# Banded attention's queries as block products, and a block's last modulation sums moved into a feed-forward

## The reference, cut to what matters

```
cond = silu(c)
for i in range(2):
    mod = cond @ w_ada[i] + b_ada[i]                       # 6 x 1024 values
    sh1, sc1, gt1, sh2, sc2, gt2 = split(mod, 6)
    h = rmsnorm(x, g_mix[i]) * (1 + sc1) + sh1
    y = mla(h, ...) if i == 0 else swa(h, ...)
    x = x + gt1 * y
    h = rmsnorm(x, g_mlp[i]) * (1 + sc2) + sh2
    x = x + gt2 * (square(relu(h @ w_ff1[i])) @ w_ff2[i])

def swa(h, w_qkv, b_qkv, sinks, w_o, b_o):
    qkv = h @ w_qkv + b_qkv      # 1024 query columns, 256 of keys, 256 of values
    ...                          # scores in a band of 128 tokens, ALiBi bias, sinks, softmax, values
    return o @ w_o + b_o
```

## Time and profile before

| | |
|---|---|
| three runs, us | 3033.01, 3033.98, 3034.07 |
| span of the profiled execution, us | 3027.7 |
| TensorE busy | 2908.8 us, 96% |
| VectorE busy | 1656.7 us, 55% |
| ScalarE busy | 722.1 us, 24% |
| GpSimd busy | 71.7 us, 2% |
| mean granted TensorE clock | 0.991 of 2.4 GHz |
| transfers | 451.73 MB, mean 149 GB/s |

### The profile page before, as it was taken

How to read it: one execution, slowest core, us unless ns; L and a number is a source line. 1 busy time by engine, 2 the same in 40 slices (tenths; PEclk the granted TensorE clock), 3 DMA queues, 4 the chain that set the end, 5 groups by cost and what they waited for, 6 DMA issues and landing times.

```text
span 3027.7 us, 36246 instructions
## 1 busy us (share of the span) xinstructions
PE 2908.8 (96%) x14418; PEld 2184.0 (72%) x14418; DVE 1656.7 (55%) x2729; ACT 722.1 (24%) x1393; POOL 71.7 (2%) x136
## 2 busy tenths in 40 slices
PE   7999999999899999989999999999999998999998
PEld 5988888788557888844444434478888846888887
DVE  4777887365666677621111157464555467655545
ACT  4444444220672001111011022420000116200001
POOL 0000000000000111000000001000000020000000
PEclk9999999999999999999999999999999999999999
DMA  5100111021103555379999967012222270122221
GB/s 236 70 36 35 65 41 56 35 91 56 67 12 104 211 184 219 118 326 421 422 422 422 422 265 319 28 56 84 84 84 84 112 279 29 56 84 93 101 85 56
DMA packets 71751, 451.73 MB, mean 149 GB/s; under 512 B 8032, under 2 KB 10224, under 8 KB 24112
## 3 DMA queue, kind: packets, MB, share of 16 engines
q1 hardware_dynamic: 53840, 374.17, 30.9%
q0 software_dynamic: 17040, 73.18, 6.7%
q10 hardware_dynamic: 720, 2.29, 0.2%
HBM read 445.41 MB, written 2.10 MB: 148 GB/s over the span
## 4 chain that ended last, share of the span: by engine, by line
PE 85%; DVE 8%; DVEq 2%; DMA 2%; ACT 2%; issue 1%; ACTq 0%; SPq 0%
PE PS L253 78%; PE PS L1671 1%; PE PS L1556 1%; PE PS L1654 1%; DVE arena L1621 1%; DVE stat L1680 1%; DVEq L1124 1%; DMA hT<-stream 1%; PE PS L2451 1%; DMA ring<-stream 1%; DMA arena<-x 1%; PE PS L2431 1%; ACT arena L1574 0%; DVE arena L1120 0%; DVE PS L2782 0%
## 5 line engine op out<-in xcount | busy, mean ns | idle before, releaser
L253 PE MATMUL PS<-arena 128*128 128x256 f32 (+3 forms) x4960 | 982.6, 388 | 17.0 <-DVE arena L1162 8.5
L253 PEld LDWEIGHTS PS<-arena 128*128 128x128 f32 (+1 forms) x4960 | 742.8, 183 | 232.4 <-issue 146.9
L253 PE MATMUL PS<-arena,ring 128*128 128x256 f32 (+1 forms) x1992 | 466.9, 390 | 0.0
L253 PEld LDWEIGHTS PS<-arena,ring 128*128 128x128 f32 x1992 | 377.8, 190 | 73.8 <-issue 25.5
L253 PE MATMUL PS<-hT,ring 128*128 128x256 f32 (+1 forms) x1504 | 400.6, 421 | 7.2 <-ACT hT L420 6.2
L253 PEld LDWEIGHTS PS<-hT,ring 128*128 128x128 f32 x1504 | 284.4, 190 | 110.5 <-issue 77.9
L253 PE MATMUL PS<-xT,arena 128*128 128x256 f32 x1056 | 232.4, 379 | 0.0
L253 PEld LDWEIGHTS PS<-xT,arena 128*128 128x128 f32 x1056 | 200.5, 190 | 31.5 <-issue 4.8
L2203 DVE TENSOR_TENSOR arena<-arena,PS 128x512 f32<-128x512 f32 x16 | 11.0, 687 | 370.1 <-PE PS L253 370.1
L253 PE MATMUL PS<-hT,arena 128*128 128x256 f32 (+1 forms) x864 | 195.1, 442 | 0.8 <-DMA hT<-stream 0.8
L597 DVE CUSTOM_DVE_ANT_0 arena<-arena,PS 128x1024 f32<-128x1024 f32 x128 | 152.1, 1217 | 43.0 <-DMA arena<-adat 41.2
(11 more groups left out here) (312 smaller groups left out, 3018.3 us busy)
## 6 DMA issues: line engine op xcount, KB each, us to landing
ring<-stream SPq DMA_DIRECT2D x217, 1024.0 KB, 7.1
arena<-stream SPq DMA_DIRECT2D x98, 1024.0 KB, 18.3
arena<-adat POOLq DMA_DIRECT2D x88, 512.0 KB, 4.9
hT<-stream SPq DMA_DIRECT2D x32, 1024.0 KB, 18.7
arena<-adat POOLq DMA_DIRECT2D x20, 1024.0 KB, 10.8
arena<-stream SPq DMA_DIRECT2D x8, 512.0 KB, 4.4
arena<-x ACTq DMA_DIRECT2D x4, 512.0 KB, 15.3
xT<-stream SPq DMA_DIRECT2D x2, 1024.0 KB, 20.9
```

The source lines that it names most:

```text
L253: ins = nc.tensor.matmul(out_, lhsT, rhs, start=start, stop=stop_, **kw)
```

## The change

Two things are changed.

The projection of banded attention does its keys and values first, as plain products (two key tiles, two of values), and then the queries as two quads (numbers N_SQ and N_SQ + 1, with the activations' differences T_s). ScalarE writes one corner of each with its bias, VectorE the other three (`query_ends`). The stream's units are put in that order. The bias table of attention (16 small instructions) moves from the start of `swa_qkv_dve` to behind the middle sums of the second query quad.

Stage 3 of the modulation rows moves into the end of layer 0's feed-forward: VectorE does 9, 10, 9 and 4 steps in its quads 12, 13, 14 and 15, between the next quad's weight sums and the accumulation. The four buffers move to the place of the first weight's activation differences, which are done with by then, and GpSimd issues the first tile when twelve quads are done, all 32 ahead of the two constant loads. The condition row is no longer made a second time: ScalarE copies stage 2's row out of PSUM into SBUF (`cond_act`, in latent attention's projection), and stages 2 and 3 read that.

Beside that, the three attentions share one set of eight semaphores, with counts that go on from one to the next.

```diff
-           [24064 + 2048 * i for i in range(4)], [23040 + 1024 * i for i in range(4)])
-MOD_DIAG = (27648, 5120, 22016, 21504)
+           [24064 + 2048 * i for i in range(4)], [20480 + 1024 * i for i in range(4)])
+MOD_DIAG = (27648, 5120, 22016)
...
+        cond = pt[:, :, :].rearrange("p a b -> p (a b)")
+        def cond_act(act):
+            act.wait_ge(m_sum, 3)
+            act.wait_ge(x_ok, 2)
+            nc.scalar.activation(cond, PS[:, MOD_BANK[2]:MOD_BANK[2] + 2, :].rearrange("p a b -> p (a b)"), ACT.Copy)\
+                .then_inc(m_sum, 1)
         def mod_steps(v, st, i0, n):
-            if i0 == 0:
-                v.wait_ge(m_sum, st + 1)
+            if i0 == 0 and st < 3:
+                v.wait_ge(m_sum, st + 1 + st // 2)
...
-                row = PS[:, MOD_BANK[st]:MOD_BANK[st] + 2, :].rearrange("p a b -> p (a b)")
+                row = cond if st >= 2 else PS[:, MOD_BANK[st]:MOD_BANK[st] + 2, :].rearrange("p a b -> p (a b)")
...
             small_squares(act, 5, ckv, KVT)
+            cond_act(act)
             take(2)
...
+        N_LATE, LATE_STEPS = 12, (9, 10, 9, 4)
...
                 if n + 1 < QF:
                     weight_sums(v, q + 1, u + 2)
-                elif L == 0:
-                    mod_diag(v, 3)
+                if L == 0 and n >= N_LATE:
+                    i = n - N_LATE
+                    mod_steps(v, 3, sum(LATE_STEPS[:i]), LATE_STEPS[i])
                 v.drain()
...
         def swa_qkv_pe(pe):
-            pe.wait_ge(n_r, NR[8] + 2)
-            mod_sum(pe, 3)
-            for j in range(12):
-                g, su = G_SQKV + j, U_SQKV + 2 * min(j // 4, 2)
-                if j < 10:
-                    gemm(pe, g, g, su, 0, ((j % 4) * P,), hT, ready=NM[8] if j == 0 else None)
+            for j in range(4):
+                g = G_SQKV + j
+                if j < 2:
+                    gemm(pe, g, g, U_SQKV, 0, (j * P,), hT, ready=NM[8] if j == 0 else None)
                 else:
-                    t0 = (j - 10) * 2 * P
-                    gemm_tok(pe, g, g, su, hT, (t0, t0 + P), 256, 256)
-                if j in (3, 7, 11):
-                    pend[0] += 2
+                    t0 = (j - 2) * 2 * P
+                    gemm_tok(pe, g, g, U_SQKV, hT, (t0, t0 + P), 256, 256)
+            pend[0] += 2
+            pe.wait_ge(evac_done, G_SQKV + 4)
+            for n in (N_SQ, N_SQ + 1):
+                for i in range(1, 8):
+                    part_pe(pe, n, i)
+                quad_done(n)
             flush(pe)
...
+        def query_ends(v, n):
+            j = 4 * (n - N_SQ)
+            u0, u1 = part_u(n, 0), part_u(n, 1)
+            def biased(j0, cols, src):
+                for t in range(2):
+                    ins = nc.vector.scalar_tensor_tensor(qn[:, j0 + t, cols], u1[:, t, :],
+                                                         V[:, V_BQKV + j0 + t:V_BQKV + j0 + t + 1], src[:, t, :],
+                                                         ALU.add, ALU.add)
+                return ins
+            v.drain()
+            biased(j + 2, slice(HN, T), u0)
+            v.wait_ge(p_p, 7 * n + 6)
+            biased(j, slice(HN, T), part_bank(1)).then_inc(p_d, 1)
+            v.wait_ge(p_p, 7 * n + 7)
+            biased(j + 2, slice(0, HN), part_bank(2)).then_inc(p_d, 1)
         def swa_qkv_dve(v):
-            for n in range(16):
-                nc.vector.tensor_scalar(BT[:, n // 4, n % 4, :], C[:, C_DIST:C_DIST + 2 * P],
-                                        C[:, C_SLOPE + n:C_SLOPE + n + 1], None, ALU.mult)
-            mod_steps(v, 3, 0, 32)
+            v.wait_ge(n_mod, NM[8] + KT)
+            block_sums(v, hT, T_s)
+            sums_dve(v, N_SQ)
             mod_end(v, 3, ((6, 80, V_GMLP + 8),))
...
+            for n in (N_SQ, N_SQ + 1):
+                last_sum_dve(v, n)
+                mid_dve(v, n, 0)
+                mid_dve(v, n, 1)
+                if n == N_SQ:
+                    sums_dve(v, n + 1)
+                else:
+                    for i in range(16):
+                        nc.vector.tensor_scalar(BT[:, i // 4, i % 4, :], C[:, C_DIST:C_DIST + 2 * P],
+                                                C[:, C_SLOPE + i:C_SLOPE + i + 1], None, ALU.mult)
+                query_ends(v, n)
             v.drain().then_inc(v_ok, 1)
...
-            pool.wait_ge(q_p, 7 * 14)
-            tiles(96, 100)
+            pool.wait_ge(q_p, 7 * 12)
+            tiles(96, 128)
             pool.wait_ge(x_ok, 4)
             pool.dma_start(bvs, bv).then_inc(in_pool, 16)
             pool.dma_start(snk[:, 0, :], sinks).then_inc(in_pool, 16)
-            tiles(100, 128)
```

More of the change, by code:

```diff
@@ L56 @@
 N_MWO = N_OUT + 2
-N_SWO = N_MWO + 2
+N_SQ = N_MWO + 2
+N_SWO = N_SQ + 2
 V_SLOT = 6
@@ L682, in quad_out @@
             j = 4 * (n % 2)
-            return gt[:, j:j + 2, :], gt[:, j + 2:j + 4, :]
+            tiles = gt if n < N_SQ else qn
+            return tiles[:, j:j + 2, :], tiles[:, j + 2:j + 4, :]
         def quad_moving(n):
@@ L1516, in build, with attention @@
         MAX, NEGMAX, SUM, RECIP, SINK = range(5)
-        def attention(name, n, nh, score, chunk, dest, groups, value, outs, exp_io, norm_io, maximum, scale,
+        a_s, a_m, a_e, a_n, a_t, a_c, a_v, a_o = (sem(f"att_{x}") for x in
+            ("s", "m", "e", "n", "t", "c", "v", "o"))
+        def attention(u0, i0, o0, n, nh, score, chunk, dest, groups, value, outs, exp_io, norm_io, maximum, scale,
                       sink=False, beside=None):
-            a_s, a_m, a_e, a_n, a_t, a_c, a_v, a_o = (sem(f"{name}_{x}") for x in
-                ("s", "m", "e", "n", "t", "c", "v", "o"))
             col = lambda what, u: stat[:, what, u % 2, 0:nh]
@@ L1680, in gqa_maximum @@
             return nc.vector.tensor_reduce(neg, S[:, :, 0:HK], AX.XY, ALU.max, negate=True)
-        gqa_pe, gqa_act, gqa_dve, gqa_out, gqa_scores = attention(
-            "gqa", 64, 1, gqa_score, gqa_chunk, gqa_dest, [list(range(4 * i, 4 * i + 4)) for i in range(16)],
+        gqa_pe, gqa_act, gqa_dve = attention(
+            0, 0, 0, 64, 1, gqa_score, gqa_chunk, gqa_dest, [list(range(4 * i, 4 * i + 4)) for i in range(16)],
             gqa_value, gqa_outs, lambda u, h, S: (Pb[:, u % 2, :, :], S[:, :, 0:HK]),
@@ L1698, in build @@
         T_w = [area(14336 + 1024 * i, KH, HN) for i in range(4)]
+        T_s = [area(at, KH, HN) for at in (8192, 9216, 12288, 13312)]
         Vq = area(2048, 2, HN)
@@ L2462, in mla_maximum @@
             return nc.vector.tensor_scalar(neg, top, -float((NOPE + ROPE_D) ** -0.5), None, ALU.mult)
-        mla_att_pe, mla_att_act, mla_att_dve, mla_out, _ = attention(
-            "mla", 16, 2, mla_score, mla_chunk, mla_dest, [list(range(4 * i, 4 * i + 4)) for i in range(4)],
+        mla_att_pe, mla_att_act, mla_att_dve = attention(
+            64, 16, 8, 16, 2, mla_score, mla_chunk, mla_dest, [list(range(4 * i, 4 * i + 4)) for i in range(4)],
             mla_value, lambda it: [(qn[:, 2 * it + c, :], OB2[c]) for c in range(2)],
@@ new lines, in swa_qkv_act @@
+            for n in (N_SQ, N_SQ + 1):
+                part_copy(act, n, 0)
+                part_copy(act, n, 1)
+                act.wait_ge(p_p, 7 * n + 5)
+                for t in range(2):
+                    j = 4 * (n - N_SQ) + t
+                    ins = nc.scalar.activation(qn[:, j, 0:HN], part_bank(0)[:, t, :], ACT.Identity,
+                                               bias=V[:, V_BQKV + j:V_BQKV + j + 1])
+                ins.then_inc(p_c, 1)
+        def query_ends(v, n):
+            j = 4 * (n - N_SQ)
+            u0, u1 = part_u(n, 0), part_u(n, 1)
+            def biased(j0, cols, src):
+                for t in range(2):
+                    ins = nc.vector.scalar_tensor_tensor(qn[:, j0 + t, cols], u1[:, t, :],
[8 more added lines that the diff above has]
+            biased(j + 2, slice(0, HN), part_bank(2)).then_inc(p_d, 1)
@@ L2787, in swa_maximum @@
             return nc.vector.tensor_tensor(extra, neg, snk[:, 0, 4 * g:4 * g + 4], ALU.add)
-        swa_att_pe, swa_att_act, swa_att_dve, swa_out, _ = attention(
-            "swa", 16, 4, swa_score, swa_chunk, swa_dest, [[u] for u in range(16)], swa_value,
+        swa_att_pe, swa_att_act, swa_att_dve = attention(
+            80, 20, 16, 16, 4, swa_score, swa_chunk, swa_dest, [[u] for u in range(16)], swa_value,
             lambda u: [(qn[:, 2 * (u // NT) + k, :], OB2[k]) for k in range(2)] if u % NT == NT - 1 else [],
```

83 lines of the change are left out of this document (44 added, 39 removed).

## The result

| us | before | after |
|---|---|---|
| median of 6 runs | 3034.17 (3033.01 to 3035.21) | 3044.10 (3039.90 to 3047.51) |
| span of the profiled execution | 3027.7 | 3039.9 |
| run time of that execution | not listed | 3041.67 |

The account below looks back on a forecast made before the run. TensorE, busy 96% of 3027.7 us, was taken as the bound. Queries -6.6, late sums +17.4 and clock +2 gave +12.8, a span of 3040.5; with the carried 6.3 the forecast was 3047 us, range 3028 to 3052.

Parts of the forecast that it names:

- The sums: End of layer 0's feed-forward, quads 12 to 15: VectorE's 32 moved modulation sums wait for tile refills; +17.4 us.
- a third of the way from free to loaded: Quads 13 and 14: refills meet part of a weight load, adding 2.0 and 1.6 us to sums of 15.2 and 13.8.
- Both other bounds: Feed-forward delay: 0.5 us with every tile in time, 9.0 with no weight load in the way.
- prompt tiles: Rival, quads 12 to 15: refills ready when needed, 23.5 us of VectorE work per quad, nothing late; 3028 us, chance 0.15.
- the three cases: Tile supply: forecast 3047 us (0.62), weight loads not holding up tiles 3036 to 3038 (0.19), every refill ready 3028 (0.15).
- The price of a tile: Modulation tile of 512 KB: 3.2 us estimated from the skill; the trace's 4.0, 5.5 and 10.9 were used instead.
- The queries: Projection stage: two quads of seven products replace eight plain query tiles, -6.6 us; rival without that gain 3053, chance 0.04.
- The clock: Behind product 7 of quad 15 TensorE idles over 4.25 us, clock about 0.5 near first key products; +2 us (0 to 3.4).
- the removed diagonal and its four matmuls: nothing: Before the projection: these 1.98 us stood beside the normalisation the first matmul waits for anyway, so removal changes nothing.
- The stalls: TensorE waits for VectorE's late middle sum before product 7 in quads 14 and 15, some 5 us each.
- From span to median: Whole kernel: the runs' median was 6.3 us above the profiled span, carried over from span 3040.5 to 3047 us.

## Why the prediction was right, and where it wasn't

- *The sums.* Right, nearly step by step. The sums of quads 12, 13 and 14 took 18.5, 16.8 and 16.3 us (forecast 18.6, 17.2, 15.4), the three cycles together 92.0 (92.3), quad 15 from middle sum to the end 13.2 (13.0), in all +17.3 (+17.4). That the total agrees to a tenth is in part luck: for quads 13 and 14 the prediction put a third of the way from free to loaded, without a row for it; measured were 1.6 and 2.5 us above free for its 2.0 and 1.6. Both other bounds were found on the chip: 0.5 with prompt tiles, 8.8 for 9.0 without the loads. Which of the three cases holds is decided by the tiles: the same sums cost 0.5 us with eight buffers. The rival of prompt tiles was therefore right as a mechanism, and its 3028 was met (3027.8 and 3027.0); its condition wasn't, with four buffers.
- *The price of a tile.* The estimate by the Trainium skill, "DMA: Bandwidth & Descriptors", section on the anatomy of a DMA, was 3.2 us. The traces disagree: none of the tiles landed in less than 3.7, and the 28 refills took 5.9 in the median, 5.1 where the weight loads were cut.
- *The queries.* Right: -6.6 at equal clock (84.62 to 78.04, the latter with the four matmuls back), with the wait behind the value tiles (0.73), the bias table and the end (1.01 for 1.98) as costed.
- *The clock.* The size was right (+1.8 in the key tiles for +2, granted clock 0.77 there for "about 0.5"), the cause was not, so the size was luck. The prediction had TensorE idle longer than 4.25 us behind product 7 of quad 15, and the sums of squares and first key products slow after that. In the changed kernel TensorE idled there for 0.21 us, since its wait lay ahead of product 5, and the sums of squares ran at full speed (3.69 us). The forecast's case is seen in the kernel with the copies first: 5.55 us of idling behind product 7, the sums of squares in 5.59 us, the key tiles at full clock. The slow key tiles have another cause: two of them take 15.55 to 15.67 us, for 13.90 at full clock, also in the four kernels where TensorE doesn't stall. The step that failed is "the removed diagonal and its four matmuls: nothing". The matmuls were hidden, but they filled TensorE's wait of 2.77 us in front of the key products; put back, they gave 1.7 us at that place in both kernels tried. In the changed kernel itself they weren't put back, and three other kernels kept the full clock without them, so for it this cause is likely and not shown.
- *The stalls.* Product 7 of quad 14 as forecast (4.27 for "some 5"). In quad 15 the stall was 9.33, before product 5: the prediction counted a square ahead of quad 15's middle sum and overlooked that ScalarE's copies for product 5 stand behind the same squares. It cost nothing in this kernel. With six buffers it cost 2.6 us by an estimate from two traces: VectorE's middle sum came at 2419.86, its work from there takes 11.7 us with eight buffers and would have ended at 2431.5; the end was 2434.16.
- *From span to median.* The rest of the miss of 2.9 us. The sum of the parts on the span was 12.8 for a measured 12.2 (0.6 of it). The other 2.3 is the carried 6.3 (6.5 as rounded): after, the median is 4.2 above the span. Each run time listed for a profiled execution is some 1.8 above its span (3041.67 for 3039.9), so the profiled execution of before was near 3029.5, low among its runs (3027.9 to 3036.1 over all that are on record), and that of after 2.4 below its median. So carrying over the 6.3 was the second step that failed: by the 1.8, some 4.5 of it were one fast execution of before, not a fixed cost. Parts that no experiment here aims at move as much: attention to the end takes 515.9 to 519.7 us in the traces of this case, and quad 12's middle sum stands at 2331.8 to 2336.9 in those of the changed kernels. The 3 us by which the kernel with short loads came out under its expected 3037 are not its key tiles: they ran at full clock (13.97 us), but 3037 had no loss of clock in it. Its span is 3.4 us above that of before, as its stages add up to, while its median equals that of before; so these 3 us lie between one profiled execution and the other runs too, and no run says more.

## What to carry to other kernels

Work that fits into an engine's idle time fits only if its operands do: count how many lie ready, take the landing time of a refill from the trace with the other loads of that stage in flight, and compare that with the time in which the ready ones are used up. Here four ready tiles gave 4.6 us of cover, and the other five or six of a quad had to come as refills of 4 to 11 us; eight gave 9.2 us, and only the last one or two of a quad had to come while its sums ran. The same 32 sums cost 17 us or 0.5. The median landing time alone doesn't decide it: with eight buffers it was 9.5 us, more than the cover, but most of those refills had until the next quad. Before removing work that is hidden, ask whether it keeps an engine from idling.

## What the runs showed of the hardware

Refills took 5.9, 8.4 and 9.5 us in the median with four, six and eight buffers, and yet with eight none was waited for. Cutting the weight loads beside them brought the slowest of 28 refills from 10.5 to 6.2 us, the median only from 5.9 to 5.1. The modulation sum took 1.22 us with its row in SBUF, as out of PSUM. Behind a wait of 2.77 us TensorE's granted clock was 0.77 to 0.81 over the next 7.3 us in seven of ten kernels and 1.00 in three; with the longest gap at 1.05 us it was 1.00 in both kernels tried.
